# Expert blocks of two sizes in a one-core transformer kernel: up to 64 tokens with high and low rows side by side

## The chip, the core and the metric

The kernel runs as one program on 1 core of a Trainium2 chip. The metric is device time in microseconds (us) for one execution. The engines are named as the profile names them: PE multiplies matrices (PEld is its load of the stationary operand), DVE, ACT and POOL work elementwise, SP and the queues ACTq and POOLq issue transfers. POOL is also called GpSimd.

## The reference

All of it is float32: 256 tokens of width 1024 pass through an attention block and then through a hybrid layer that ends in a mixture of experts. The change touches only that last part:

```python
scores = jax.nn.sigmoid((t @ w_router).astype(jnp.float32))
_, eidx = lax.top_k(scores + router_bias, 8)          # 8 of 64 experts for each token
g = take_along_axis(scores, eidx, 1); g = g / sum(g) * 2.5
...                                                   # tokens sorted by expert, in blocks of up to 128
def expert_block(e, toks, gs):
    xb = t[toks]
    return (silu(xb @ w1[e]) * (xb @ w3[e])) @ w2[e] * gs[:, None]
out = routed_sum(expert_block) + swiglu(t, ws1, ws3, ws2)
```

`w1` and `w3` are 1024x256 for each expert, `w2` is 256x1024: 3 MB an expert. Evaluated on its own inputs, the reference's routing gives 33 experts any token at all: 17 of them have more than 64 tokens (69 to 124), 16 have 1 to 59, none has more than 128.

## The kernel before

Two thirds of the span are the attention block, the mixing layer and the router; the change leaves them alone. Then the routing code (DVE, L1596 to L1622) counts the tokens of each (expert, half) pair, drops the empty ones and writes a list `work`: the number of blocks, the expert of each, and the column of the table `pcol` that holds its gates and ranks. One block is one expert with up to 128 tokens, 33 of them. They run in a loop that each engine has as a program of its own, unrolled over r = 0 to 3; i is the block's number, and semaphores alone tie the engines together.

To keep float32 accuracy at a fast matmul rate, each operand is split into a high part (`_hi`, rounded by ACT) and a rest (`_lo`, a subtraction on DVE), and a product is three matmuls: hi*hi, hi*lo, lo*hi. For block i:

- PE, "up" (L2074): 8 pieces of 128 rows of w1 and w3 side by side, three products each, 24 matmuls of 512 columns into `hidden_b`. Then it transposes (turns) the gathered rows of block i+1 (L2051, 8 transposes), adds block i-1's result to the output sums (scatter, L2059, two halves of 4 matmuls), turns h (L2089, 2 transposes) between the halves, finds the tokens of block i+2 (L2041), and does "down" (L2101, 12 matmuls).
- ACT: `down_hi` (L1166), two pieces of `up_hi` of block i+1 (L1149), silu (L1174), the high part of the next rows (L1144), `h_hi` (L1177), the other two pieces of `up_hi`, `y_hi` (L1185).
- DVE: two `down_lo` (L1667), two `up_lo` (L1642), the product with silu (L1672), the rest of the next rows (L1636), `h_lo` (L1675), gates and tokens (L1628, L1629), two more `up_lo`, two `y_lo` (L1684).
- POOL: `pick` (L899), a comparison that selects the tokens of block i+2; `put` (L929), the matrix that scatters block i's rows, from a row of `place_rows` that SP broadcast to all partitions (L754); and the gather of 128 rows of block i+2 from DRAM (L909).
- SP: loads the weights of block i+2 into the buffer that block i leaves free (L742, L749), after DVE's last `down_lo` of block i.

## Time and profile before

| | us |
|---|---|
| median of 3 runs | 1058.93 |
| lowest, highest | 1056.66, 1059.56 |
| span of the profiled execution | 1053.0 |
| first matmul of block 0, first matmul of block 32 | 656.73, 1029.93 |

The span runs from the first instruction to the last; the time of a run also holds what lies around it. The page gives busy time per engine. Lists by window give, for a stretch, the busy us and the number (x) of instructions of PE, PEld, DVE, ACT and POOL, the granted PE clock (1.00 is 2.4 GHz, 0.5 is 1.2 GHz), the share of the 16 transfer engines and GB/s. A timeline row gives the start, the duration, engine, line, operation, output<-inputs, shape and how many instructions stand in the row (x2). In brackets is the idle time before it and who ended it. A matmul's duration is from start to its last result; the next one starts before that, so the rate is read from the starts.

### The profile page before, as it was taken

How to read it: one execution, taken by the hardware profiler on the slowest of the kernel's cores; microseconds unless marked ns; L12 is line 12 of the kernel's file. 1: busy time of each engine (PE TensorE's matmuls, PEld its weight loads, DVE VectorE, ACT ScalarE, POOL GpSimd, SP SyncE). 2: the span in 40 equal slices, each digit the busy share in tenths (PEclk: the TensorE clock that was granted, in tenths of full speed). 3: DMA queues.
4: the chain of work that ended last, by engine and by line, in shares of the span. 5: the costliest groups of instructions: out<-in, count | busy, mean ns of one | idle time of the engine just before them, and what ended most of it. 6: DMA issues, size and time to landing. Idle time of an engine off the chain costs nothing. (4 is left out here: it accounts for less than half of the span.)

```text
span 1053.0 us, 16530 instructions
## 1 busy us (share of the span) xinstructions
PE 1003.7 (95%) x5182; PEld 810.2 (77%) x5182; DVE 787.6 (75%) x1310; ACT 584.7 (56%) x895; POOL 287.9 (27%) x355
## 2 busy tenths in 40 slices
PE   8999999999999899989879989999999999999996
PEld 7778777778766676778768876778888888888885
DVE  4677888768844543566775654899999999999997
ACT  4554664445433342435425423777777777777774
POOL 5154452224100000041226113322322232233222
PEclk9999999999999999999989999999999999999999
DMA  9877777768635243536242316888888888788884
GB/s 315 277 260 257 225 237 274 234 201 283 211 99 180 96 160 120 171 93 232 88 153 88 101 60 259 313 307 321 341 327 313 334 332 329 306 340 341 325 314 179
DMA packets 85349, 247.39 MB, mean 235 GB/s; under 512 B 13276, under 2 KB 23957, under 8 KB 71986
## 3 DMA queue, kind: packets, MB, share of 16 engines
q1 hardware_dynamic: 71042, 201.19, 53.3%
q0 software_dynamic: 13680, 45.13, 12.0%
q8 instruction: 29, 0.48, 0.2%
q10 hardware_dynamic: 576, 0.41, 0.1%
q14 instruction: 22, 0.18, 0.1%
HBM read 244.27 MB, written 2.29 MB: 234 GB/s over the span
## 5 line engine op out<-in xcount | busy, mean ns | idle before, releaser
L1804 PE MATMUL bank<-w_hi,a_hi 128*128 128x512 f32 (+2 forms) x512 | 205.3, 401 | 10.0 <-DVE w_lo L1266 4.5
L1804 PE MATMUL bank<-w_hi,a_lo 128*128 128x512 f32 (+2 forms) x512 | 196.5, 384 | 0.0
L1804 PE MATMUL bank<-w_lo,a_hi 128*128 128x512 f32 (+2 forms) x512 | 196.2, 383 | 0.0
L1266 DVE TENSOR_TENSOR w_lo<-ring,w_hi 128x1024 fp32r<-128x1024 f32 (+2 forms) x132 | 152.7, 1181 | 50.4 <-ACT w_hi L989 46.5
L989 ACT ACTIVATE w_hi<-ring 128x1024 fp32r<-128x1024 f32 (+2 forms) x140 | 141.0, 1023 | 73.9 <-PE bank L1804 70.2
L1642 DVE TENSOR_TENSOR up_lo<-raw_weights,up_hi 128x1024 fp32r<-128x1024 f32 x136 | 164.4, 1250 | 3.0
L1149 ACT ACTIVATE up_hi<-raw_weights 128x1024 fp32r<-128x1024 f32 x136 | 135.8, 1050 | 0.1
L1804 PEld LDWEIGHTS bank<-w_hi,a_hi 128*128 128x128 f32 x512 | 96.2, 188 | 39.4 <-issue 17.6
L1804 PEld LDWEIGHTS bank<-w_hi,a_lo 128*128 128x128 f32 x512 | 96.2, 188 | 19.8
L1804 PEld LDWEIGHTS bank<-w_lo,a_hi 128*128 128x128 f32 x512 | 96.4, 188 | 18.2 <-issue 1.4
L2074 PE MATMUL bank<-up_hi,x_block_hi 128*128 128x512 f32 x264 | 105.1, 398 | 1.0 <-issue 1.0
L2074 PE MATMUL bank<-up_lo,x_block_hi 128*128 128x512 f32 x264 | 104.9, 397 | 0.0
L2074 PE MATMUL bank<-up_hi,x_block_lo 128*128 128x512 f32 x264 | 104.9, 397 | 0.0
L929 POOL TENSOR_SCALAR put<-block_rows,consts 128x256 fp32r<-128x256 f32 x33 | 30.5, 924 | 246.6 <-PE bank L2059 127.4
L820 POOL DMA_DIRECT2D merged<-in_w_ada_dram x96 | 53.2, 557 | 127.4 <-DVE ada_acc L1405 94.1
L800 POOL TENSOR_SCALAR mean_squares<-mean_squares 128x8 f32<-128x8 f32 (+2 forms) x32 | 10.4, 325 | 279.0 <-ACT logits L942 199.0
L1667 DVE TENSOR_TENSOR down_lo<-raw_weights,down_hi 128x1024 fp32r<-128x1024 f32 x66 | 77.9, 1222 | 7.3 <-ACT down_hi L1166 7.2
L1405 DVE SCALAR_TENSOR_TENSOR ada_acc<-merged,c_col,ada_acc 128x512 f32<-128x512 f32 x84 | 62.8, 748 | 6.4 <-DMA merged<-in_w_ada_dram 3.5
L1166 ACT ACTIVATE down_hi<-raw_weights 128x1024 fp32r<-128x1024 f32 x66 | 66.0, 1050 | 0.3 <-issue 0.3
L1185 ACT ACTIVATE y_hi<-bank,block_gates 128x512 fp32r<-128x512 f32 x66 | 45.5, 689 | 31.3 <-PE bank L2101 30.9
L2074 PEld LDWEIGHTS bank<-up_hi,x_block_hi 128*128 128x128 f32 x264 | 50.0, 189 | 13.2 <-issue 1.2
L2074 PEld LDWEIGHTS bank<-up_hi,x_block_lo 128*128 128x128 f32 x264 | 50.1, 190 | 12.0
(264 smaller groups left out, 1926.5 us busy)
## 6 DMA issues: line engine op xcount, KB each, us to landing
raw_weights<-in_w_dram SPq DMA_DIRECT2D x102, 1024.0 KB, 7.0
ring<-in_w_in_dram SPq DMA_DIRECT2D x58, 1024.0 KB, 5.8
merged<-in_w_ada_dram POOLq DMA_DIRECT2D x96, 256.0 KB, 4.2
ring<-in_w_out_dram SPq DMA_DIRECT2D x8, 1024.0 KB, 5.9
ring<-in_w_branch_dram SPq DMA_DIRECT2D x6, 1024.0 KB, 4.9
bias<-rel_rows SPq DMA_DIRECT2D x40, 128.0 KB, 5.2
block_rows<-place_rows SPq DMA_DIRECT2D x34, 128.0 KB, 8.7
ring<-in_ws_dram SPq DMA_DIRECT2D x2, 1024.0 KB, 5.3
```

The source lines that it names most:

```text
L820: gp.dma_start(ada_row(q), src).then_inc(S(f"ada_loaded_{q % ADA_SLOTS}"), 16)
L929: gp.tensor_scalar(put[:, :], row4[:, r, :], consts[:, C_COL:C_COL + 1], None, ALU.is_equal)\
L989: act.activation(w_parts[0][:, 2 * p:2 * p + 2, 0:w], view(j, kind)[:, 2 * p:2 * p + 2, :], ACT.Copy)\
L1149: act.activation(up_hi[:, r % 2, 4 * kh:4 * kh + 4, m, :], raw_up(raw[:, 1 - r % 2, :], kh, m), ACT.Copy)\
L1166: act.activation(down_hi[:, f, :], raw[:, 1 - r % 2][:, UP + f * DM:UP + (f + 1) * DM], ACT.Copy)\
L1185: act.activation(y_hi[:, hf * CH:(hf + 1) * CH], y_b[hf][:, :], ACT.Copy, scale=gcol[:, r, 0:1])\
L1266: dve.tensor_tensor(w_parts[1][:, 2 * p:2 * p + 2, 0:w], view(JOB[it[1:3]], kind)[:, 2 * p:2 * p + 2, :], w_parts[0][:, 2 * p:2 * p + 2, 0 ...
L1405: dve.scalar_tensor_tensor(out=o, in0=ada_row(q), scalar=c_col[:, 1, k:k + 1], in1=o, op0=ALU.mult, op1=ALU.add) .then_inc(S("ada_step" if ...
L1642: dve.tensor_tensor(up_lo[:, r % 2, 4 * kh:4 * kh + 4, m, :], raw_up(raw[:, 1 - r % 2, :], kh, m), up_hi[:, r % 2, 4 * kh:4 * kh + 4, m, : ...
L1667: dve.tensor_tensor(down_lo[:, f, :], raw[:, 1 - r % 2][:, UP + f * DM:UP + (f + 1) * DM], down_hi[:, f, :].bitcast(F32), ALU.subtract).th ...
L1804: mm = pe.matmul(ps[:, 0:wide], a_parts[za][:, k, t * P:(t + 1) * P], w_parts[zw][:, k, 0:wide], start=start, stop=stop)
L2074: mm = pe.matmul(hidden_b[:, :], (xe_hi, xe_lo)[zx][:, k, :], (up_hi, up_lo)[zw][:, r % 2, k].rearrange("p m n -> p (m n)"), start=(k == 0 ...
```

## The change

Blocks alternate. A block with an even number takes up to 128 tokens, as before. A block with an odd number ("half") takes up to 64: its rows are gathered as 64, and the high part stands in columns 0 to 63 and the rest in columns 64 to 127 of one stationary operand. So two matmuls (with `up_hi`, with `up_lo`) stand in for three, 16 instead of 24 in "up" and 8 instead of 12 in "down". After "up", rows 64 to 127 of the result have to be added to rows 0 to 63 (an ACT copy to `hidden_sum`, a DVE addition). The routing sorts experts into large and small and interleaves them: large ones at even places, small ones at odd places; what is left of the longer list follows. An odd place with no small expert would run as an empty block. `put` is now made from the token column `tok_f` and a constant row, so `place_rows`, its broadcast and the transposes that made it are gone. One of the four `up_lo` pieces of each block moves from DVE to POOL, behind the gather. In a half block both halves of the scatter come before the transposes of h.

The core of the diff (DVE and PE helpers in the order of the file):

```diff
+HALF = P // 2
+UP_PIECES = ((0, 0), (0, 1), (1, 0))
...
-                sp.dma_start(row4[:, r, :], place_rows[bass.ds(v, 1), :].to_broadcast([P, TOK])).then_inc(S(f"row_loaded_{r}"), 16)
...
+                at = S_HALF if r % 2 else S_TOK
                 for t in range(NT):
-                    gp.tensor_scalar(pick[:, r % 2, t, :], consts[:, C_IOTA:C_IOTA + P], col4[:, r, 4 * t + 3:4 * t + 4].bitcast(F32), None, ALU.is_equal)\
+                    gp.tensor_scalar(pick[:, r % 2, t, :], slots[:, at:at + P], col4[:, r, 4 * t + 3:4 * t + 4].bitcast(F32), None, ALU.is_equal)\
                       .then_inc(S("pick_ready"), 1)
...
+                rows = HALF if r % 2 else P
+                gp.indirect_dma_start(out=xg[0:rows, r % 2, :], out_offset=None, in_=h2_rows,
+                                      in_offset=bass.IndirectOffsetOnAxis(ap=tok[0:rows, r, 0:1], axis=0))\
                   .then_inc(S(f"rows_gathered_{r}"), 16)
+
+            def rest_of_up_weights(i, r):
+
+                gp.wait_ge(S("up_hi"), 4 * i + 4)
+                gp.sem_inc(S("begun"), 1)
+                gp.tensor_tensor(up_lo[:, r % 2, KT // 2:KT, 1, :], raw_up(raw[:, 1 - r % 2, :], 1, 1),
+                                 up_hi[:, r % 2, KT // 2:KT, 1, :].bitcast(F32), ALU.subtract).then_inc(S("up_lo_pool"), 1)
...
-                        gp.wait_ge(S(f"row_loaded_{r}"), 16 * (m4 + 1))
-                        gp.sem_inc(S("pool_begun"), 1)
-                        gp.tensor_scalar(put[:, :], row4[:, r, :], consts[:, C_COL:C_COL + 1], None, ALU.is_equal)\
+                        gp.sem_inc(S("begun"), 1)
+                        gp.tensor_scalar(put[:, :], slots[:, S_TOK:S_TOK + TOK], tok_f[:, r, 0:1], None, ALU.is_equal)\
                           .then_inc(S("put_ready"), 1)
-                        gather_rows(i + 2, after)
+                        gather_rows(i + 2, after, m4 * (BODY // 2) + (r + 2) // 2)
+                        rest_of_up_weights(i + 1, (r + 1) % BODY)
...
+                        rows = HALF if r % 2 else P
+                        if r % 2:
+                            act.wait_ge(S("up_done"), i + 1)
+                            act.activation(hsum[0:HALF, :], hidden_b[HALF:P, :], ACT.Copy).then_inc(S("half_low_copied"), 1)
+                            act.wait_ge(S("half_summed"), m4 * (BODY // 2) + (r // 2 + 1))
+                            gated = hsum[0:HALF, 0:ED]
+                        else:
+                            act.wait_ge(S("up_done"), i + 1)
+                            gated = hidden_b[:, 0:ED]
+                        act.activation(hs[0:rows, 0, :], gated, ACT.Silu).then_inc(S("silu_done"), 1)
+                        round_rows(nxt, m4 * (BODY // 2) + (r + 1) // 2)
                         act.wait_ge(S("h_turned"), i + 1)
-                        act.activation(h_hi[:, :, :], turned_b[:, 0:ED].rearrange("p (f n) -> p f n", f=FT), ACT.Copy)\
-                           .then_inc(S("h_hi_ready"), 1)
+                        act.activation(h_hi[:, :, 0:rows], turned_b[:, 0:FT * rows].rearrange("p (f n) -> p f n", f=FT),
+                                       ACT.Copy).then_inc(S("h_hi_ready"), 1)
...
+                    chain(dve.tensor_scalar(used[:, :], counted, consts[:, C_THR:C_THR + 1], None, ALU.is_gt))
+                    chain(dve.tensor_scalar(kinds[:, 0:1], counted, consts[:, C_THR:C_THR + 1], float(HALF), ALU.subtract,
+                                            ALU.is_gt))
+                    dve.tensor_tensor(kinds[:, 1:2], used[:, :], kinds[:, 0:1], ALU.subtract).then_inc(S("used_ready"), 1)
...
+                    large, small = place[:, 0:1], place[:, 1:2]
+                    n_large, n_small = place[:, 2:3], place[:, 3:4]
+                    chain(dve.tensor_scalar(used_at[:, 0:1], small, 1.0, n_large, ALU.add, ALU.min))
+                    chain(dve.tensor_tensor(used_at[:, 0:1], used_at[:, 0:1], small, ALU.add))
+                    chain(dve.scalar_tensor_tensor(out=used_at[:, 1:2], in0=large, scalar=2.0, in1=used_at[:, 0:1],
+                                                   op0=ALU.mult, op1=ALU.subtract))
+                    chain(dve.scalar_tensor_tensor(out=used_at[:, 1:2], in0=used_at[:, 1:2], scalar=kinds[:, 0:1],
+                                                   in1=used_at[:, 0:1], op0=ALU.mult, op1=ALU.add))
+                    dve.tensor_scalar(order[:, :], consts[:, C_IOTA:C_IOTA + NV], used_at[:, 1:2],
                                       used[:, 0:1], ALU.is_equal, ALU.mult).then_inc(S("order_ready"), 1)
...
-                    dve.wait_ge(S("ranks_turned"), 1)
-                    dve.tensor_copy(prow[:, :], y_b[0][:, 0:TOK]).then_inc(S("rows_turned"), 1)
+                        chain(dve.tensor_copy(pcol[:, 0:NV, 4 * t + 3], ranks[:, t, :]))
+                    chain(dve.tensor_scalar(n_blocks[:, :], place[0:1, 2:3], 2.0, -1.0, ALU.mult, ALU.add))
+                    dve.scalar_tensor_tensor(out=work[0:1, 0:1], in0=place[0:1, 3:4], scalar=place[0:1, 2:3],
+                                             in1=n_blocks[:, :], op0=ALU.add, op1=ALU.max).then_inc(S("work_ready"), 1)
...
+                dve.tensor_copy(tok_f[:, r, :], hidden_b[:, 2:3]).then_inc(S("gates_ready"), 1)
...
+                if r % 2:
+                    dve.wait_ge(S("half_x_hi_ready"), pair + 1)
+                    dve.tensor_tensor(xe_hi[:, :, HALF:P], y_b[0][:, :].rearrange("p (b n) -> p b n", b=KT),
+                                      xe_hi[:, :, 0:HALF].bitcast(F32), ALU.subtract).then_inc(S("half_x_lo_ready"), 1)
+                    return
...
+                if half:
+                    dve.wait_ge(S("half_low_copied"), pair(0) + 1)
+                    dve.tensor_tensor(hsum[0:HALF, :], hidden_b[0:HALF, :], hsum[0:HALF, :], ALU.add)\
+                       .then_inc(S("half_summed"), 1)
                 dve.wait_ge(S("silu_done"), i + 1)
-                dve.tensor_tensor(he, hs[:, 0, :], hidden_b[:, ED:2 * ED], ALU.mult).then_inc(S("h_done"), 1)
-                rest_of_rows(i + 1)
+                dve.tensor_tensor(he[0:rows], hs[0:rows, 0, :], (hsum if half else hidden_b)[0:rows, ED:2 * ED], ALU.mult)\
+                   .then_inc(S("h_done"), 1)
+                rest_of_rows(nxt, pair(1))
                 dve.wait_ge(S("h_hi_ready"), i + 1)
-                dve.tensor_tensor(h_lo[:, :, :], turned_b[:, 0:ED].rearrange("p (f n) -> p f n", f=FT),
-                                  h_hi[:, :, :].bitcast(F32), ALU.subtract).then_inc(S("h_lo_ready"), 1)
+                dve.tensor_tensor(h_hi[:, :, HALF:P] if half else h_lo[:, :, :],
+                                  turned_b[:, 0:FT * rows].rearrange("p (f n) -> p f n", f=FT),
+                                  h_hi[:, :, 0:rows].bitcast(F32), ALU.subtract).then_inc(S("h_lo_ready"), 1)
                 take_tokens(i + 2, (r + 2) % BODY)
-                for m in range(2):
-                    rest_of_up_weights(i + 1, nxt, 1, m)
+                rest_of_up_weights(i + 1, nxt, 1, 0)
...
+                if r % 2:
+                    pe.sem_inc(S("begun"), 1)
+                    for k in range(KT):
+                        mm = pe.transpose(y_b[0][:, k * HALF:(k + 1) * HALF], xg[0:HALF, r % 2, k * P:(k + 1) * P],
+                                          consts[0:HALF, C_ID:C_ID + HALF])
+                    mm.then_inc(S("half_rows_turned"), 1)
+                    return
...
+                if half:
+                    pe.wait_ge(S("half_x_lo_ready"), pair(0) + 1)
                 for k in range(KT):
                     if k % 4 == 0:
-                        pe.wait_ge(S(f"x_lo_ready_{k // 4}"), i + 1)
-                        pe.wait_ge(S("up_lo"), 4 * i + k // 2 + 2)
-                    for n, (zx, zw) in enumerate(PASSES):
+                        if not half:
+                            pe.wait_ge(S(f"x_lo_ready_{k // 4}"), pair(0) + 1)
+                        pe.wait_ge(S("up_lo"), 3 * i + k // 4 + 2)
+                    if k == 4:
+                        pe.wait_ge(S("up_lo_pool"), i + 1)
+                    passes = PASSES[0:2] if half else PASSES
+                    for n, (zx, zw) in enumerate(passes):
                         mm = pe.matmul(hidden_b[:, :], (xe_hi, xe_lo)[zx][:, k, :],
                                        (up_hi, up_lo)[zw][:, r % 2, k].rearrange("p m n -> p (m n)"),
-                                       start=(k == 0 and n == 0), stop=(k == KT - 1 and n == 2))
+                                       start=(k == 0 and n == 0), stop=(k == KT - 1 and n == len(passes) - 1))
...
+                    if half:
+                        scatter(1, i).then_inc(S("block_done"), 1)
...
+                    pe.wait_ge(S("h_lo_ready"), i + 1)
                 for hf in range(2):
-                    pe.wait_ge(S(f"x_lo_ready_{hf}"), i + 2)
-                    for n, (f, zh, zw) in enumerate(DOWN_PASSES):
-                        if hf == 0 and n == 2 * FT:
+                    if half:
+                        pe.wait_ge(S(f"x_lo_ready_{hf}"), pair(1) + 1)
+                    elif hf == 0:
+                        pe.wait_ge(S("half_x_lo_ready"), pair(1) + 1)
+                    passes = DOWN_PASSES[0:2 * FT] if half else DOWN_PASSES
+                    for n, (f, zh, zw) in enumerate(passes):
+                        if not half and hf == 0 and n == 2 * FT:
                             pe.wait_ge(S("h_lo_ready"), i + 1)
                         mm = pe.matmul(y_b[hf][:, :], (h_hi, h_lo)[zh][:, f, :],
                                        (down_hi, down_lo)[zw][:, f, hf * CH:hf * CH + CH],
-                                       start=(n == 0), stop=(n == len(DOWN_PASSES) - 1))
+                                       start=(n == 0), stop=(n == len(passes) - 1))
```

On DVE, one trip of the loop before, with the semaphores each row waits for (`hT` is h before it is turned):

```order
L1667 TENSOR_TENSOR down_lo<-raw_weights,down_hi 128x1024 [waits down_hi]
...
L1642 TENSOR_TENSOR up_lo<-raw_weights,up_hi 128x4x256 [waits up_hi]
L1672 TENSOR_TENSOR hT<-hs,bank 128x256 [waits silu_done]
L1634 REGISTER_ALU
L1636 TENSOR_TENSOR x_block_lo<-bank,x_block_hi 128x512 [waits x_hi_ready_0]
L1636 TENSOR_TENSOR x_block_lo<-bank,x_block_hi 128x512 [waits x_hi_ready_1]
L1675 TENSOR_TENSOR h_lo<-bank,h_hi 128x256 [waits h_hi_ready]
```

And in a half block of the changed kernel, the same place:

```order
L1687 TENSOR_TENSOR up_lo<-raw_weights,up_hi 128x4x256 [waits up_hi]
L1718 ISA
L1719 TENSOR_TENSOR hidden_sum<-bank,hidden_sum 64x512 [waits half_low_copied]
L1722 TENSOR_TENSOR hT<-hs,hidden_sum 64x256 [waits silu_done]
L1679 ISA
L1681 TENSOR_TENSOR x_block_lo<-bank,x_block_hi 128x512 [waits x_hi_ready_0]
L1681 TENSOR_TENSOR x_block_lo<-bank,x_block_hi 128x512 [waits x_hi_ready_1]
L1726 TENSOR_TENSOR h_hi<-bank,h_hi 128x2x64 [waits h_hi_ready]
```

The addition stands behind the two `up_lo` and ahead of the product; the rows of the next block, a full one, still come ahead of h's rest.

On PE, from the transposes of h to "down" in a half block (both halves of the scatter stand ahead of the first row here):

```order
L2156 MATMUL bank<-consts,hT 128x64 [waits h_done]
L2156 MATMUL bank<-consts,hT 128x64
L2087 ISA
L2089 MATMUL bank<-block_cols,pick 128x4 [waits pick_ready]
L2089 MATMUL bank<-block_cols,pick 128x4
L2162 ISA [waits h_hi_ready]
L2167 ISA [waits h_lo_ready,down_lo]
L2174 MATMUL bank<-down_hi,h_hi 128x512 [waits x_lo_ready_0]
```

"Down" of a half block waits for h's rest before its first matmul; before, the wait for it stood at the fifth. On POOL, one trip of the changed loop, with a new last row:

```order
L903 TENSOR_SCALAR pick<-slots,block_cols 128x128 [waits tokens_product]
L903 TENSOR_SCALAR pick<-slots,block_cols 128x128
L941 TENSOR_SCALAR put<-slots,block_tokens_f 128x256 [waits slots_loaded,block_done]
L909 REGISTER_ALU [waits h2_stored]
L911 ISA [waits tokens_ready]
L914 DMA x_gathered<-h_rows,block_tokens 64x1024 [waits half_rows_turned]
L920 ISA
L922 TENSOR_TENSOR up_lo<-raw_weights,up_hi 128x4x256 [waits up_hi]
```

The next `pick` stands behind that piece.

## Rows read from the trace of the kernel before

**Rows 1.** The page: span, and busy time by engine.
```profile
span 1053.0 us, 16530 instructions
PE 1003.7 (95%) x5182; PEld 810.2 (77%) x5182; DVE 787.6 (75%) x1310; ACT 584.7 (56%) x895; POOL 287.9 (27%) x355
```
**Rows 2.** Line L2074, "up": count, durations, first and last start.
```profile
L2074 PE MATMUL bank<-up_hi,x_block_lo x264: 388/397/628, 657.7 to 1035.3; 128*128 128x512 f32 x132
```
**Rows 3.** By window: the first matmuls, then the loop.
```profile
656.70:660.20 3.50, 3.47 (x8) 2.81 (x9) 2.96 (x4) 3.50 (x4) 0.00 (x0) 0.51 1.01 415
660.20:1029.90 369.70, 368.00 (x1777) 301.76 (x1776) 341.23 (x444) 281.50 (x380) 115.25 (x125) 1.00 0.85 325
```
**Rows 4.** Timeline of PE over one block, 797.7 to 810.
```profile
797.78 0.39 PE L2074 MATMUL bank<-up_hi,x_block_hi 128*128 128x512 f32 x1
...
803.37 1.05 PE L2051 MATMUL bank<-consts,x_gathered 128*128 128x128 f32 x8
804.18 0.47 PE L2059 MATMUL bank<-y_hi,put 128*128 128x512 f32 x1
...
805.20 0.39 PE L2089 MATMUL bank<-consts,hT 128*128 128x128 f32 x2
...
806.49 0.48 PE L2101 MATMUL bank<-down_hi,h_hi 128*128 128x512 f32 x1
...
809.34 0.39 PE L2074 MATMUL bank<-up_hi,x_block_hi 128*128 128x512 f32 x1
```
**Rows 5.** The same block on ACT, DVE, POOL and SP.
```profile
799.68 2.36 DVE L1667 TENSOR_TENSOR down_lo<-raw_weights,down_hi 128x1024 fp32r<-128x1024 f32 x2 [0.23 <-ACT down_hi L1166]
...
801.96 2.35 DVE L1642 TENSOR_TENSOR up_lo<-raw_weights,up_hi 128x1024 fp32r<-128x1024 f32 x2
...
802.87 0.82 SPq L742 DMA_DIRECT2D raw_weights<-in_w_dram  x2
...
803.57 0.38 ACT L1174 ACTIVATE hs<-bank 128x256 f32<-128x256 f32 x1 [1.07 <-PE bank L2074]
...
804.02 1.09 ACT L1144 ACTIVATE x_block_hi<-bank 128x512 fp32r<-128x512 f32 x2
...
804.24 0.41 DVE L1672 TENSOR_TENSOR hT<-hs,bank 128x256 f32<-128x256 f32 x1
...
804.65 1.29 DVE L1636 TENSOR_TENSOR x_block_lo<-bank,x_block_hi 128x512 fp32r<-128x512 f32 x2
...
805.62 0.38 ACT L1177 ACTIVATE h_hi<-bank 128x256 fp32r<-128x256 f32 x1 [0.51 <-PE bank L2089]
...
806.04 0.42 DVE L1675 TENSOR_TENSOR h_lo<-bank,h_hi 128x256 fp32r<-128x256 f32 x1
...
807.78 1.37 POOL L909 DMA_INDIRECT x_gathered<-h_rows,block_tokens  x1 [0.16 <-issue]
```
**Rows 6.** POOL's rest of weights beside DVE, around 526.
```profile
524.20 9.61 POOL L859 TENSOR_TENSOR w_lo<-ring,w_hi 128x1024 fp32r<-128x1024 f32 x4 [6.08 <-ACT w_hi L989]
```
**Rows 7.** DVE there, and line L1561 in all.
```profile
526.69 2.37 DVE L1561 TENSOR_TENSOR selmask<-score,consts 128x128 f32<-128x128 f32 x1
L1561 DVE TENSOR_TENSOR selmask<-score,consts x2: 431/1398/2365, 526.7 to 539.8; 128x128 f32<-128x128 f32 x1, 128x256 f32<-128x256 f32 x1
```
**Rows 8.** Block 1: POOL's picks beside DVE's weight work; one late pick.
```profile
671.11 4.77 POOL L899 TENSOR_SCALAR pick<-consts,block_cols 128x128 fp32r<-128x128 f32 x2
...
673.05 2.45 DVE L1642 TENSOR_TENSOR up_lo<-raw_weights,up_hi 128x1024 fp32r<-128x1024 f32 x2
```
**Rows 9.** Waits over the loop, 660 to 1043: PE's for gathered rows.
```profile
PEld bank L2051 <- DMA x_gathered<-h_rows,block_tokens: 7.2, 20, 1.0
```
**Rows 10.** Transfers from 804 to 812, then from 812 to 815, by queue.
```profile
q1 hardware_dynamic: 412, 3.07, 96.0%
...
q0 software_dynamic: 144, 0.52, 43.0%
```
**Rows 11.** DVE in the routing: a small step, and the copy for `place_rows`.
```profile
633.10 0.22 DVE L1596 TENSOR_SCALAR used<-bank,consts 128x1 f32<-128x1 f32 x1 [0.99 <-PE bank L2019]
...
637.57 0.42 DVE L1619 COPY prow<-bank 128x256 f32<-128x256 f32 x1
```

More of the change, by code:

```diff
@@ L512, in build @@
         ranks = sb("ranks", [P, NT, NV], F32, routing)
[L513 removed]
         gsum = sb("gsum", [P, NT], F32, routing)
         used = sb("used", [NV, 1], F32, routing)
[L516 removed]
+        kinds = sb("kinds", [NV, 2], F32, routing)
+        used_at = sb("used_at", [NV, 2], F32, routing)
+        place = sb("place", [NV, 4], F32, routing)
+        n_blocks = sb("n_blocks", [1, 1], F32, routing)
         order = sb("order", [NV, NV], F32, routing)
@@ L1655, in _, with expert_block @@
             take_tokens(1, 1)
-            for kh in range(2):
-                for m in range(2):
-                    rest_of_up_weights(0, 0, kh, m)
-            rest_of_rows(0)
-            dve.wait_ge(S("work_ready"), 2)
+            for kh, m in UP_PIECES:
+                rest_of_up_weights(0, 0, kh, m)
+            rest_of_rows(0, 0)
+            dve.wait_ge(S("work_ready"), 3)
             n_work = dve.value_load(work[0:1, 0:1], min_val=0, max_val=MAX_WORK)
-            def expert_block(i, r):
+            def expert_block(i, r, pair):
                 nxt = (r + 1) % BODY
+                half = r % 2
+                rows = HALF if half else P
                 for f in range(FT):
@@ L2085, in expert_block @@
                     scatter(0, i)
+                    if half:
+                        scatter(1, i).then_inc(S("block_done"), 1)
                 pe.wait_ge(S("h_done"), i + 1)
+                rows = HALF if half else P
+                if half:
+                    pe.sem_inc(S("begun"), 1)
                 for f in range(FT):
-                    mm = pe.transpose(turned_b[:, f * P:(f + 1) * P], he[:, f:ED:FT], ident)
+                    mm = pe.transpose(turned_b[:, f * rows:(f + 1) * rows], he[0:rows, f:ED:FT], consts[0:rows, C_ID:C_ID + rows])
                 mm.then_inc(S("h_turned"), 1)
-                if not first:
+                if not first and not half:
                     scatter(1, i).then_inc(S("block_done"), 1)
```

133 lines of the change are left out of this document (68 added, 65 removed).

## The prediction

> **What bounds the kernel now.** I read the page first: PE is busy 95% of the span [rows 1]. The change sits in the block loop, so the next view is line L2074: its first and last starts are 377.6 us apart, which is 32 blocks and 21 matmuls (21 x 0.23), so a block takes (377.6 - 4.9)/32 = 11.65 us on average [rows 2]. The window of the loop says who fills it: PE 368.0 of 369.7 us, DVE 341.2 (92%), ACT 281.5, the transfer engines 0.85 [rows 3]. PE is the bound, and DVE and the transfers stand close behind, so less PE work pays only as far as these let it.
>
> The timeline of one block gives the budget [rows 4]. From 797.78 to 809.34 are 11.56 us: "up" 24 matmuls in 5.59 (0.233 each), transposes of rows 0.81, then 2.31 with 8 scatter matmuls, h's transposes and the token search, "down" 12 matmuls in 2.85 (0.2375 each). The 0.09 us to the mean are blocks in which PE waits for gathered rows, 7.2 us in 20 waits, most of them in the first blocks [rows 9].
>
> The same block on the others is the view that decides [rows 5]. Times are from the block's first matmul. DVE starts `down_lo` at +1.90, because ACT must first round the last block's y and then `down_hi`. Four subtractions follow without a gap, and the product with silu starts at +6.46, though silu was done at +6.17. So in a full block DVE is already level with PE there: the transposes of h stand at +7.42.
>
> **The change part by part.** The reference's routing has 17 experts above 64 tokens and 16 below. They interleave exactly: 33 blocks as before, 17 full and 16 half, none empty.
>
> *Half block, PE alone.* 16 x 0.233 + 0.81 + 2.31 + 8 x 0.2375 = 8.75 us, 2.8 less than now. If that were all, 16 halves would save 45 us.
>
> *Half block, the chain through DVE.* The start at +1.90 and the four subtractions stay, since the piece that went to POOL is the fourth of `up_lo`, which lies later. So the new addition cannot start before +6.46, while PE has ended "up" at +3.7. From there, each step by its nearest row [rows 5]: addition of 64x512, as one of the two `x_block_lo`, 0.65; silu 0.38; product 0.41; with some 0.1 of handover this is +8.0. DVE then does the rows of the next full block, 1.29, which ends at +9.35 (ACT's 1.09 behind silu keeps ahead of it). h's transposes and `h_hi` lie inside that: PE to ACT took 0.42 (805.20 to 805.62), `h_hi` under 0.38. h's rest, half as wide as the 0.42 of today, is 0.3: +9.65, and PE can begin "down" at +9.75. 1.90 more gives **11.65 us**. The ACT copy of rows 64 to 127 (about 0.6) lies in ACT's present gap before silu and costs nothing; without that gap it would add its 0.6. Bounds: 11.3, if the 64-partition steps are shorter by a third and handovers vanish, and 12.1, if each of the seven handovers costs 0.1 more than I allow.
>
> *Picks.* POOL's next `pick` pair now runs behind the piece, so beside DVE's subtractions instead of ahead of them. That was seen once, in block 1: the picks took 4.77 us for two, and DVE's two `up_lo` 2.45 instead of 2.35 [rows 8, 5]. I take twice 0.1 for the two, +0.2 on the half block: 11.85. The picks end near +7 and PE asks for them after +8, so their own lateness is covered.
>
> *Full block.* It keeps all products. The rows that it turns are the 64 of the next half: 8 transposes of 64 columns instead of 128, 0.81 to some 0.55; bounds 0.4 and 0.81. The addition does not occur, `x_block_lo` is one step instead of two. 11.56 - 0.26 = **11.3 us** (11.15 to 11.56).
>
> *Transfers.* Today 3.07 MB of weights go by themselves at 96% until 812, and the gather's 0.52 MB comes behind them by 815 [rows 10]. The issue at +5.1 hangs on DVE, so it stays. Without the broadcast and with every second gather halved, the load falls from 0.85 of the time. The rows of a full block are wanted at +3.7 of the half before it and land near +4.9, but that half waits for DVE until +8.0 anyway. The waits of [rows 9] should nearly vanish.
>
> *POOL's piece.* 2.4 us each [rows 6]. It starts behind the gather, about +11.2, and ends near +2.1 of the next block. PE wants it at its ninth or thirteenth "up" matmul, +1.9 in a half (slack there), +2.8 in a full block. What it does to DVE is in the trace: beside four such pieces in a row a DVE operation of two SBUF inputs took 2.37 us where a wider one of the same line took 0.43, and the wait was as long as the piece beneath it [rows 6, 7]. So whichever comes second waits. DVE's `down_lo` wants to start at +1.9, about when the piece lets go. I take 0 for it, and put the risk in a rival.
>
> The Trainium skill, SBUF — State Buffer, section "SBUF: two separate sides", says that the pair of ports shared by VectorE and GpSimd is an exclusive lock held for a whole instruction, between a VectorE operation with two SBUF inputs and a GpSimd one that reads SBUF. The 2.37 us of [rows 7] agrees. By that rule DVE would wait for the last 0.2 to 0.3 us of every piece, 33 x 0.25 = 8 us on top of the sum.
>
> *Routing.* Before the first block, eight small DVE steps come in (kinds, places, number of blocks) at 0.22 each, one behind the other, and the copy of 0.42 goes [rows 11]. They lie on the path to `work`, whose readers start the first weights: +1.3 us (bounds 0.8 and 2).
>
> *Sum.* 16 pairs of 11.3 + 11.85 = 370.4 against 32 x 11.65 = 372.8: -2.4. With the routing +1.3: -1.1. The profiled execution, 1053.0, would have a span of 1051.9; the runs stand 5.9 above that span in their median, so I forecast **1057.8 us**: no change that can be told, since 0.3% (3.2 us) is about what a measurement tells from none.
>
> **The rivals.**
>
> *A. The half block becomes what PE needs (faster).* If DVE's start moved forward, a half would fall to DVE's own work in it (341.2 us over the 31.7 blocks of [rows 3] are 10.8 each, less 1.2 for the piece, plus 0.65 for the addition: 10.2). 16 x 1.65 = 26 less: 1033. For it: PE's 2.8 us. Against: DVE's first subtraction follows ACT's `down_hi`, which follows the end of "down"; nothing in the change shortens this. A weak form, both bounds low (11.15 + 11.3 + 0.1): 16 x 0.75 = 12 less, +1.3, so 1048. Together 0.25.
>
> *B. POOL's piece and DVE collide (slower).* Its place is the start of a block, its price the piece's 2.4 us or a part. It decides when the gather ends after +11.4, or when a half falls below 11.5: then the piece still runs at +1.9 and all four subtractions, the addition and "down" shift with it. If it comes even later, DVE's subtractions are already running, and POOL has to wait for them as the picks did [rows 8], and PE for `up_lo_pool`. At 0.5 us a block it costs 33 x 0.5 = 16: 1074. At 1 us in halves and fulls alike, 1091. For it: the margin is only some 0.1 us. Against: DVE works on PSUM just while the piece runs. 0.23.
>
> *C. Longer handovers (slower).* The upper bound of the half, 12.1 + 0.2, and 11.56 for the full: 16 x 0.56 = 9, +1.3: 1069. Between that and the sum lies 1063. 0.12.
>
> *D. The clock.* In the half PE idles some 3 us, in two or three pieces. The granted clock was 0.51 from 656.7 to 660.2, behind a start with long gaps, and 1.00 in all of the loop [rows 3]. If a half fell to 1.2 GHz for 3.5 us, it would lose about half of that: 16 x 1.7 = 27, 1086. No single gap should be above 1.3 us. 0.03.
>
> *E. The lists don't interleave.* With one large expert fewer the blocks stay 33; with each two more, an empty half of 11.85 us comes in. The router rounds as before; 0.01.
>
> **How the numbers follow.** The forecast 0.36, A 0.25, B 0.23, C 0.12, D and E 0.04. The likeliest one's own range is 1054 to 1063. The range that should hold 8 in 10 leaves out the strong form of A and the heavy collisions: 1044 to 1078. Faster by over 0.3%: A and the lower edge of the forecast's own range, 0.28. Within 0.3%: 0.32. Slower by over 0.3%: B, C, D, E and the upper edge, 0.40.
>
> **What would show it.** In the profile after: 16 matmuls of "up" in every second block, the period alternating 11.3 and 11.85; in a half, DVE's addition at +6.5 and PE idle ahead of h's transposes and again ahead of "down"; `up_lo` on POOL of 2.4 us ending before DVE's `down_lo`. I am wrong if the addition starts well before +6.4, if `down_lo` starts past +2.1 or takes over 1.4 us for one, if POOL's piece starts past the next block's start, or if the granted clock in the loop is below 1.

## The result, and the profile after

| | before | after |
|---|---|---|
| median of 4 runs | 1059.1 | 1095.8 |
| lowest, highest | 1056.66, 1059.56 | 1092.33, 1097.52 |
| block loop (first matmul of block 0 to that of block 32) | 373.2 | 411.4 |
| behind the loop | 23.0 | 22.3 |

The ratio is 1.0347 (95%: 1.0325 to 1.037): slower. Forecast was 1057.8, with a range up to 1078. The two medians differ by 36.7 us, the two profiled executions by 42.7 (1053.0 and 1095.7). Of these 38.2 lie in the loop. The first matmul of block 0 also stands 5.2 us later: 3.5 of them arise ahead of the routing, in code that the change leaves alone, and most of that is one stretch at 1.2 GHz (from 352.8 on) that the execution of before did not have; 1.7 come from the routing on.

The page of the changed kernel, the same lines as [rows 1] (a group's last numbers are busy us and mean ns of one):
```profile
span 1095.7 us, 16111 instructions
PE 998.1 (91%) x4988; PEld 785.8 (72%) x4988; DVE 766.2 (70%) x1317; ACT 583.8 (53%) x894; POOL 403.8 (37%) x391
...
L1713 DVE TENSOR_TENSOR down_lo<-raw_weights,down_hi 128x1024 fp32r<-128x1024 f32 x66 | 91.7, 1428 | 7.2 <-ACT down_hi L1184 7.2
```
PE has 194 matmuls less than before and only 5.6 us less busy time. The 192 matmuls of "up" and "down" that are gone would be 45 us at before's 0.233 us each, so the others take longer than they did. The window of the loop, with the columns of [rows 3], gives one reason: the mean granted clock is 0.93 where before had 1.00. (The "up" matmuls with the rest of the rows number 136, which is 17 x 8: there are 17 full blocks and 16 halves, as forecast, and rival E is out.) Then four stretches of one block's end and the next one's start:
```profile
661.92:1073.30 411.38, 362.77 (x1592) 278.85 (x1593) 322.53 (x448) 283.49 (x382) 226.66 (x159) 0.93 0.73 276
...
936.30:939.90 3.60, 2.96 (x16) 2.26 (x16) 3.04 (x4) 1.08 (x4) 0.49 (x2) 1.00 0.57 177
939.90:943.28 3.38, 2.21 (x10) 1.84 (x11) 2.88 (x7) 2.83 (x6) 1.41 (x2) 1.00 1.01 427
943.28:946.68 3.40, 3.40 (x9) 2.64 (x8) 2.13 (x3) 2.86 (x4) 3.37 (x3) 0.50 1.04 377
946.68:950.00 3.32, 3.32 (x16) 2.67 (x15) 3.32 (x4) 2.18 (x3) 2.46 (x2) 1.00 0.08 15
```
From 943.28 to 946.68 the granted clock is 0.50 (1.2 GHz): 9 matmuls where the next stretch has 16. Ahead of it PE was idle for a third of one stretch (2.21 us busy of 3.38) and a fifth of the one before. There are 16 such stretches of 3.4 us in the loop, 54.6 us in all; before had one, in block 0, where the changed kernel has one too.

Now the half block that ends there, beside [rows 4, 5], from the timeline of the changed kernel. Its PE:
```profile
931.17 0.40 PE L2136 MATMUL bank<-up_hi,x_block_hi 128*128 128x512 f32 x1
...
933.46 0.50 PE L2136 MATMUL bank<-up_hi,x_block_hi 128*128 128x512 f32 x1 [0.26 <-POOL up_lo L922]
...
936.30 1.09 PE L2106 MATMUL bank<-consts,x_gathered 128*128 128x128 f32 x8 [0.71 <-DMA x_gathered<-h_rows,block_tokens]
...
939.97 0.42 PE L2156 MATMUL bank<-consts,hT 64*128 64x64 f32 x2 [0.70 <-DVE hT L1722]
...
941.80 0.49 PE L2174 MATMUL bank<-down_hi,h_hi 128*128 128x512 f32 x1 [1.10 <-DVE h_hi L1726]
...
944.14 0.63 PE L2136 MATMUL bank<-up_hi,x_block_hi 128*128 128x512 f32 x1
```
And POOL and DVE of the same stretch:
```profile
929.66 1.30 POOL L914 DMA_INDIRECT x_gathered<-h_rows,block_tokens  x1 [0.21 <-issue]
...
931.00 2.41 POOL L922 TENSOR_TENSOR up_lo<-raw_weights,up_hi 128x1024 fp32r<-128x1024 f32 x1
...
933.04 2.92 DVE L1713 TENSOR_TENSOR down_lo<-raw_weights,down_hi 128x1024 fp32r<-128x1024 f32 x2 [0.20 <-ACT down_hi L1184]
933.36 2.99 POOL L903 TENSOR_SCALAR pick<-slots,block_cols 128x128 fp32r<-128x128 f32 x2
...
935.88 2.44 DVE L1687 TENSOR_TENSOR up_lo<-raw_weights,up_hi 128x1024 fp32r<-128x1024 f32 x2
...
938.25 0.67 DVE L1719 TENSOR_TENSOR hidden_sum<-bank,hidden_sum 64x512 f32<-64x512 f32 x1
...
941.23 0.28 DVE L1726 TENSOR_TENSOR h_hi<-bank,h_hi 128x128 fp32r<-128x128 f32 x1
...
943.78 2.40 POOL L922 TENSOR_TENSOR up_lo<-raw_weights,up_hi 128x1024 fp32r<-128x1024 f32 x1
```
In offsets from 931.17: `down_lo` starts at +1.87, as forecast, but POOL's piece runs until +2.24, and the two subtractions take 2.92 us where [rows 5] has 2.36. The addition stands at +7.08 (forecast 6.46), h's transposes at +8.80, "down" at +10.63 (forecast 9.75). PE idles at four places. Three of them come back in every half, the one for the gathered rows in most. The waits over the loop of the changed kernel (us in total, times, longest):
```profile
PE bank L2156 <- DVE hT L1722: 19.4, 19, 1.6
PE bank L2174 <- DVE h_hi L1726: 17.4, 16, 1.1
PE bank L2136 <- POOL up_lo L922: 6.1, 16, 2.1
PE bank L2106 <- DMA x_gathered<-h_rows,block_tokens: 5.1, 9, 1.0
...
PEld bank L2106 <- DMA x_gathered<-h_rows,block_tokens: 11.2, 15, 1.4
```
Before had none of the first three. The last row is the one to hold against [rows 9] (7.2 us in 20 waits): the wait for gathered rows has grown, and it now stands in the halves.

The routing did what was forecast. `used` to `work` is 6.41 us, where before had 5.28, so +1.1 (forecast 1.3); from `work` to the first matmul it is 0.6 more. The first small step, as in [rows 11]:
```profile
636.56 0.22 DVE L1622 TENSOR_SCALAR used<-bank,consts 128x1 f32<-128x1 f32 x1 [0.99 <-PE bank L2071]
```

### The profile page after: what moved, and what is told of

Read it like the earlier page. It is cut to its first block and busy times, and to the rows that moved or that the text cites. A ratio compares the mean times of both kernels' runs of the same rounds, so it can differ in the third digit from the quotient of the medians.

```text
span 1095.7 us, 16111 instructions
## 1 busy us (share of the span) xinstructions
PE 998.1 (91%) x4988; PEld 785.8 (72%) x4988; DVE 766.2 (70%) x1317; ACT 583.8 (53%) x894; POOL 403.8 (37%) x391
## 3 DMA queue, kind: packets, MB, share of 16 engines
q0 software_dynamic: 12656, 40.87, 11.3%
## 5 line engine op out<-in xcount | busy, mean ns | idle before, releaser
L1687 DVE TENSOR_TENSOR up_lo<-raw_weights,up_hi 128x1024 fp32r<-128x1024 f32 x102 | 126.5, 1267 | 0.9 <-ACT up_hi L1167 0.5
L2136 PE MATMUL bank<-up_hi,x_block_hi 128*128 128x512 f32 x264 | 109.9, 416 | 8.2 <-POOL up_lo L922 6.1
L2136 PE MATMUL bank<-up_lo,x_block_hi 128*128 128x512 f32 x264 | 108.0, 409 | 0.0
L1713 DVE TENSOR_TENSOR down_lo<-raw_weights,down_hi 128x1024 fp32r<-128x1024 f32 x66 | 91.7, 1428 | 7.2 <-ACT down_hi L1184 7.2
L903 POOL TENSOR_SCALAR pick<-slots,block_cols 128x128 fp32r<-128x128 f32 x70 | 87.4, 1260 | 22.4 <-DMA block_cols<-pcol 22.4
L1735 DVE SCALAR_TENSOR_TENSOR y_lo<-bank,block_gates,y_hi 128x512 fp32r<-128x512 f32 x66 | 49.5, 751 | 52.4 <-ACT y_hi L1211 52.2
L922 POOL TENSOR_TENSOR up_lo<-raw_weights,up_hi 128x1024 fp32r<-128x1024 f32 x34 | 81.8, 2406 | 0.9
L941 POOL TENSOR_SCALAR put<-slots,block_tokens_f 128x256 fp32r<-128x256 f32 x33 | 31.4, 953 | 134.2 <-issue 134.2
L2174 PE MATMUL bank<-down_hi,h_hi 128*128 128x512 f32 x132 | 64.1, 486 | 18.0 <-DVE h_hi L1726 17.4
L2136 PEld LDWEIGHTS bank<-up_hi,x_block_hi 128*128 128x128 f32 x264 | 52.5, 199 | 27.8 <-POOL up_lo L922 13.0
```

Of the source, the lines that this page charges most:

```text
L903: gp.tensor_scalar(pick[:, r % 2, t, :], slots[:, at:at + P], col4[:, r, 4 * t + 3:4 * t + 4].bitcast(F32), None, ALU.is_equal)\
L922: gp.tensor_tensor(up_lo[:, r % 2, KT // 2:KT, 1, :], raw_up(raw[:, 1 - r % 2, :], 1, 1), up_hi[:, r % 2, KT // 2:KT, 1, :].bitcast(F32), ...
L1687: dve.tensor_tensor(up_lo[:, r % 2, 4 * kh:4 * kh + 4, m, :], raw_up(raw[:, 1 - r % 2, :], kh, m), up_hi[:, r % 2, 4 * kh:4 * kh + 4, m, : ...
L1713: dve.tensor_tensor(down_lo[:, f, :], raw[:, 1 - r % 2][:, UP + f * DM:UP + (f + 1) * DM], down_hi[:, f, :].bitcast(F32), ALU.subtract).th ...
L1735: dve.scalar_tensor_tensor(out=y_lo[:, c], in0=y_b[hf][:, :], scalar=gcol[:, r, 0:1], in1=y_hi[:, c].bitcast(F32), op0=ALU.mult, op1=ALU.s ...
L2136: mm = pe.matmul(hidden_b[:, :], (xe_hi, xe_lo)[zx][:, k, :], (up_hi, up_lo)[zw][:, r % 2, k].rearrange("p m n -> p (m n)"), start=(k == 0 ...
```

## The experiments

Theory after the comparison: (1) POOL's piece (the `up_lo` subtraction that moved there) and DVE hold each other up, about 0.6 us a block; (2) the idle time that this leaves in halves makes the clock fall, and that costs some 15 us more; (3) without both the half block would be near its forecast. Rivals: the clock alone does it; the half's chain through DVE alone; the new `put`. All times below are medians; the loop is that of the profiled execution. "Full" and "half" are the two kinds of block, and lengths of blocks are the usual ones. Ratios are to the kernel before on the same chip.

**e2_no_piece.** The changed kernel, with the fourth piece of `up_lo` on DVE again.
```diff
-UP_PIECES = ((0, 0), (0, 1), (1, 0))
+UP_PIECES = ((0, 0), (0, 1), (1, 0), (1, 1))
...
-                        rest_of_up_weights(i + 1, (r + 1) % BODY)
```


> The changed kernel with the fourth up_lo piece given back to DVE (POOL has pick, put and gather alone). Theory 1 (piece and DVE collide): DVE's two down_lo take 2.36 again instead of 2.7 to 2.9, the addition of the half starts at +6.5 instead of +7.1, the waits of PE for up_lo on POOL (19 us in sum, 32 times) go, the half is 11.9 or less at full clock and there are fewer stretches at 1.2 GHz: 1072 to 1082. Theory 2 (the addition's chain alone, and the clock): the start of the addition moves, but PE idles as long and the clock falls as often: 1088 to 1095. Theory 3: DVE has too much to do with four pieces (10.9 a block, 11.4 in a half) and the time is above 1098.

Measured: 1067.4, ratio 1.0078 (1.0061 to 1.0095), loop 384.8: below theory 1's range. Halves take 11.92 us at full clock, fulls 11.52. One half on DVE and PE:
```profile
986.06 0.40 PE L2131 MATMUL bank<-up_hi,x_block_hi 128*128 128x512 f32 x1
...
987.93 2.36 DVE L1709 TENSOR_TENSOR down_lo<-raw_weights,down_hi 128x1024 fp32r<-128x1024 f32 x2 [0.20 <-ACT down_hi L1180]
...
992.48 0.68 DVE L1715 TENSOR_TENSOR hidden_sum<-bank,hidden_sum 64x512 f32<-64x512 f32 x1
...
994.26 1.29 DVE L1677 TENSOR_TENSOR x_block_lo<-bank,x_block_hi 128x512 fp32r<-128x512 f32 x2 [0.20 <-ACT x_block_hi L1158]
...
996.04 0.49 PE L2169 MATMUL bank<-down_hi,h_hi 128*128 128x512 f32 x1 [1.10 <-DVE h_hi L1722]
```
The addition is at +6.42, as forecast; "down" at +9.98 and not +9.75, since `x_block_lo` began 0.2 late behind ACT and the handover to PE took more. So the piece costs 28 us of the 36.7, what it does to the clock included (16 stretches at 1.2 GHz with it, 6 without). The line of `down_lo` (shortest/median/longest ns) shows the collision by itself. Without the piece:
```profile
L1709 DVE TENSOR_TENSOR down_lo<-raw_weights,down_hi x66: 1214/1222/1228, 662.6 to 1049.4; 128x1024 fp32r<-128x1024 f32 x66
```
In the changed kernel:
```profile
L1713 DVE TENSOR_TENSOR down_lo<-raw_weights,down_hi x66: 1209/1224/3473, 662.3 to 1076.4; 128x1024 fp32r<-128x1024 f32 x66
```

**e5_warm_light and e1_warm.** The changed kernel, with small matmuls that add zeros in a half, where PE waits: 2, 4 and 4 of them in the code (e1: 6, 10 and 8), ahead of the turn of the rows, of h's transposes and of "down". In the trace each stands as two matmuls of 0.11 us from start to start, so e5 adds 20 to a half (2.2 us) and e1 adds 48 (5.3 us), twice what the expectations reckon.
```diff
+                if half:
+                    stay_warm(4)
                 pe.wait_ge(S("h_done"), i + 1)
```


> The changed kernel, plus small matmuls without dependents on PE in half blocks only: 6 before the rows are turned, 10 before the transposes of h, 8 before down. They add zeros to an output sum, so only PE's idle time is filled. Theory 1 (the clock): in the profile after, PE falls to 1.2 GHz some 14 times in the loop because the half blocks leave it idle, and blocks that meet no such stretch are 12.58 (half) and 11.52 (full). With the gaps filled the granted clock stays 1.00 in the loop and 16 pairs of 24.1 to 24.4 replace the 411.4 us of the loop by 386 to 391: 1070 to 1076. Theory 2 (the chain alone): the half is bound by DVE, the slow matmuls lie in time that PE would have waited anyway, and the time stays at 1090 to 1098. Theory 3: the fillers push real work back by themselves: 24 of 0.11 us, up to 2.6 us a half where they do not fit, above 1100.

> As e1_warm with fewer fillers in the half blocks: 2, 4 and 4 instead of 6, 10 and 8 (0.11 us each as e1_warm's trace has them), few enough to fit in the idle time of the changed kernel (0.7, 0.7 and 1.1 us). Theory 1 (the clock costs the changed kernel what its slow blocks show): the granted clock stays 1.00 in the loop, halves take 12.6 to 12.9, fulls 11.5: 1073 to 1080, against 1095.8 of the changed kernel. Theory 2 (the slow stretches lie in time that is lost anyway): the clock may stay up and the time is 1090 to 1098 all the same.

Measured: e1 1112.4, ratio 1.0501; the clock stayed up but for one stretch in block 1, yet so many fillers are work themselves (halves 15.0 us), so it told nothing of the price. e5: 1081.35, ratio 1.0222 (1.0191 to 1.0253), loop 397.3, just above theory 1's range because fulls do not return to 11.5. Its loop window, and the fillers:
```profile
662.40:1059.70 397.30, 380.99 (x1912) 301.61 (x1913) 331.72 (x447) 284.20 (x382) 249.57 (x158) 1.00 0.75 285
...
L2123 PE MATMUL bank<-ones,zeros x320: 269/275/414, 680.8 to 1057.5; 128*128 128x128 f32 x160
```
With fewer stretches at 1.2 GHz (3.4 us in all) the loop is 14.1 us shorter than the changed kernel's, more matmuls notwithstanding. Of the 14.1, 1.5 are the stretch in block 0, which e5 lacks. What stays is the collision at full clock: halves 12.59, fulls mostly 12.0 to 12.3, against 11.92 and 11.52 in e2. That is 0.6 us a block, in both kinds. The fillers don't lengthen the halves: those halves of the changed kernel that kept the full clock take 12.58 to 12.61. The fulls behind them take 11.9 to 12.1 there, so up to some 2 us of e5's loop may be the fillers'.

**e3_put_only and e4_put_piece.** The kernel before, whole blocks only, with `put` built from the token column; e4 adds POOL's piece behind the gather.
```diff
-tensor_scalar(put[:, :], row4[:, r, :], consts[:, C_COL:C_COL + 1], ...)
+tensor_scalar(put[:, :], slots[:, S_TOK:S_TOK + TOK], tok_f[:, r, 0:1], ...)
...
+                        rest_of_up_weights(i + 1, (r + 1) % BODY)   # e4
```


> The kernel before with only the scatter matrix made from the token column and a constant row: no place_rows, no broadcast, no transposes of the ranks, one small DVE copy more a block. If the broadcast ahead of the gather was what PE waited for (8.2 us in 22 waits in the loop), these waits go and the loop falls by 2 to 4 us, the routing by 0.4: 1054 to 1057. If the gather is late for another reason: 1058 to 1060.

> The run before this one (scatter matrix from the token column, all 33 blocks of the full size) plus the fourth up_lo piece on POOL. Theory 1: the collision delays DVE's down_lo by 0.3 to 0.6 a block, but a full block's DVE has 0.5 of room before the transposes of h, so this is 0 to 4 us slower than that run. Theory 2: each block pays the delay: 33 x 0.5 = 16 us slower. Theory 3 (faster): DVE was the hidden bound and the piece frees it: 2 to 5 us faster.

Measured: e3 1053.5, ratio 0.9946 (0.9929 to 0.9962); e4 1062.5, ratio 1.0036 (1.0022 to 1.0049). In e3 the blocks from block 5 on are 11.55 us each and the waits of [rows 9] shrink:
```profile
PEld bank L2043 <- DMA x_gathered<-h_rows,block_tokens: 1.3, 2, 0.7
```
e4 has the collision with no half block in sight, 0.28 us a block and 9 us in all, between its theories 1 and 2:
```profile
L1673 DVE TENSOR_TENSOR down_lo<-raw_weights,down_hi x66: 1210/1392/2146, 660.8 to 1041.6; 128x1024 fp32r<-128x1024 f32 x66
```

**e6_piece_early.** The changed kernel, with the piece moved to where POOL sits idle: it takes the second piece of `up_lo` behind the picks, ahead of `put` and gather, and DVE takes the fourth.
```diff
-UP_PIECES = ((0, 0), (0, 1), (1, 0))
+UP_PIECES = ((0, 0), (1, 0), (1, 1))
...
                         make_pick(i + 2, after, m4 + 1 + (r + 2) // BODY)
+                        rest_of_up_weights(i + 1, (r + 1) % BODY)
```


> The changed kernel with another piece on POOL at another place: the second of the four up_lo pieces, behind the picks and ahead of put and gather, so it can run from +4.8 of a block, when ACT has rounded it, and not at a block's start. DVE has only three subtractions before the addition. Theory 1 (what hurt was where the piece stood, beside down_lo): no stretched down_lo (2.36), the addition of the half starts at +5.4, but its product with silu reads two SBUF inputs and can wait for the piece until +7.6, so the half is 11.5 to 12.0; DVE's work is 9.9 a block: 1050 to 1066. Theory 2 (any such piece on POOL costs DVE its own 2.25 us somewhere): 1080 or more, and DVE operations with two SBUF inputs are stretched elsewhere.

Measured: 1061.4, ratio 1.0033 (1.0001 to 1.0065), loop 373.1: 34 us less than the changed kernel, with as many subtractions on each engine in another order. `down_lo` is at 1.2 us each again. But the half still takes 11.55, though DVE reaches the addition at +5.32. The timeline of a half says why:
```profile
981.74 2.78 POOL L922 TENSOR_TENSOR up_lo<-raw_weights,up_hi 128x1024 fp32r<-128x1024 f32 x1 [3.73 <-ACT up_hi L1167]
...
983.37 1.42 DVE L1721 TENSOR_TENSOR hT<-hs,hidden_sum 64x256 f32<-64x256 f32 x1 [0.48 <-ACT hs L1200]
```
The product reads two SBUF tiles and lasts until just behind the piece's end (984.52), 1.42 us for 0.42.

**e7_piece_early_psum, e9_early_psum_only, e10_early_order_only.** e9 is e6 with the sum of the two products written back to PSUM, so addition and product have one SBUF input each; e10 is e6 with the second scatter behind h's transposes in halves too; e7 has both.
```diff
-dve.tensor_tensor(hsum[0:HALF, :], hidden_b[0:HALF, :], hsum[0:HALF, :], ALU.add)
+dve.tensor_tensor(hidden_b[0:HALF, :], hidden_b[0:HALF, :], hsum[0:HALF, :], ALU.add)
...
-                    if half:
-                        scatter(1, i).then_inc(S("block_done"), 1)
...
-                if not first and not half:
+                if not first:
                     scatter(1, i).then_inc(S("block_done"), 1)
```


> e6_piece_early, and the addition of the half writes its sum back to PSUM, so that silu and the product read PSUM and no DVE step between the third subtraction and h's rest has two SBUF inputs; and PE has h's transposes between the halves of the scatter again, as in a full block. Theory 1: addition at +5.4, product at +6.5, down at +8.7, half 10.6 to 11.0, full 11.5 (or a gather wait of up to 0.5); with the clock up 1035 to 1045, with the clock falling in halves 1045 to 1055. Theory 2: the gathered rows are late for the half (they landed near +4.9) and the transfers (0.85 busy at 11.65 us a block) bound it: half 11.3, 1048 to 1055.

> e6_piece_early with one of e7's two edits: the sum of the half block's two products is written back to PSUM, so the addition and the product with silu have one SBUF input each; TensorE's order stays as in the changed kernel. Theory P (the port): in e6 the product with silu starts at +6.5 but h's transposes come only at +8.05, because a DVE operation of two SBUF inputs waits for POOL's piece that runs beside it; e7 had them at +7.0. So this edit alone gives nearly all of e7: loop near 358 us, halves 10.8, time 1042 to 1045. Theory O (the order): the gain came from putting the second scatter behind h's transposes; then this run stays at e6, halves 11.8, time 1055 to 1062.

> e6_piece_early with the other edit of e7 alone: in a half block the second scatter comes behind h's transposes on TensorE, as in a full one; the sum stays in SBUF. Theory P: the product stays held by POOL's piece, halves 11.7 to 11.8, time 1055 to 1062 as e6. Theory O: halves 10.8 and 1042 to 1045. A third, that the second scatter did nothing but fill a gap and taking it away only moves work behind the transposes: halves up to 0.4 longer, 1062 to 1068.

| | time | ratio (95%) | loop | usual half |
|---|---|---|---|---|
| e6 | 1061.4 | 1.0033 (1.0001 to 1.0065) | 373.1 | 11.55 |
| e9 | 1051.4 | 0.9928 (0.991 to 0.9946) | 365.4 | 11.15 |
| e10 | 1056.0 | 0.9976 (0.9958 to 0.9994) | 370.6 | 11.52 |
| e7 | 1042.3 | 0.9861 (0.983 to 0.9891) | 357.7 | 10.67 |

Neither theory held alone: e9 missed theory P's 1042 to 1045, e10 fits theory P and excludes theory O. With the product free but the second scatter ahead of the transposes, PE itself was late (h's transposes at +7.87), not least because it had waited 1.0 us for the gathered rows: from one half of e9 to the next, the length follows that wait (10.97 with 0.85, 11.14 with 1.03, 12.21 with 2.09); with the order mended but the product held, DVE was (+8.03). Both together give +7.02 and 0.9 us a half, where the single edits give 0.4 and nothing. The product's line in e7 has no long case any more, though the piece runs beside it as before:
```profile
L1721 DVE TENSOR_TENSOR hT<-hs,bank x33: 411/420/423, 666.8 to 1024.5; 128x256 f32<-128x256 f32 x17, 64x256 f32<-64x256 f32 x16
```
What is left in e7's halves is nearly all one wait, for the gathered rows of the next full block; no run here moves the gather:
```profile
PE bank L2106 <- DMA x_gathered<-h_rows,block_tokens: 17.8, 16, 2.2
```
e7 is the fastest kernel of the study, 14.6 us under before (1056.9 on that chip). Its clock stays at full speed in the loop:
```profile
660.55:1018.20 357.65, 335.06 (x1592) 263.02 (x1593) 305.00 (x447) 282.57 (x383) 203.13 (x159) 1.00 0.83 315
```

**e8_no_piece_psum.** e2 with e7's two last edits: is the piece needed at all?

> e2_no_piece with the sum in PSUM and the order of PE in halves as in a full block, no piece on POOL. If the length of the half is the chain of DVE's four subtractions, addition, silu, product (e2: 11.93 at full clock), little moves: half 11.8 to 11.95. The second half of the scatter now stands in the wait for h's rest, so PE idles in other places; if the clock falls less for it, 1060 to 1064, if not 1066 to 1069.

Measured: 1062.65, ratio 1.0051 (1.0026 to 1.0076), loop 379.9, halves 11.75 at full clock. It is: DVE's fourth subtraction ahead of the addition is worth 1.1 us a half. The clock is in the difference too: e8 has five stretches at 1.2 GHz in the loop, e7 none.

**e11_put_piece_early.** e4 with the piece in e6's place, no half blocks.

> The kernel before with put from the token column (as e3_put_only) and POOL's piece, but the second of up_lo, run behind the picks as in e6, so no half blocks. It tells what of e7's gain is the halves' and what is the piece's. Theory H (the halves are what pays): all blocks full and bound by TensorE at 11.5 us, loop 368 to 370, time 1052 to 1054 as e3, so e7's further 10 us are the half blocks. Rival S (DVE's relief pays): DVE one subtraction shorter ahead of the product lets every block fall to 11.2, loop near 358, time near 1043, and the half blocks bring nothing by themselves. Rival L: the product reads one SBUF input here, but down_lo or the picks collide with the piece as in e4: 11.8 a block, 1060.

Measured: 1055.2, ratio 0.9968 (0.9954 to 0.9982), loop 370.8, blocks of 11.55 from block 5 on. Theory H: DVE's relief brings nothing where PE is the bound (ratio 0.0022 above e3's). So what e7 has over e3, 9 us by the ratios and 11.9 in the loop, is the half blocks', and they give it only with the piece in the right place.

## Why the prediction was wrong

The loop, by parts, forecast 370.4 and measured 411.4:

| part | from | us |
|---|---|---|
| fulls 11.52, not 11.3 | e2, 16 x 0.22 | +3.5 |
| halves 11.92, not 11.85 | e2, 16 x 0.07 | +1.1 |
| the piece against DVE, at full clock | e5 397.3, less 16 x (11.52 + 11.92) = 375.0 | +22.3 |
| the clock | changed kernel less e5 | +14.1 |
| sum | | 41.0 |

The table takes each kind of block at its usual length; block 0 and block 1, which differ, are in the last two parts.

*POOL's piece: the step that failed.* The sum gave the piece nothing. "I take 0 for it" rested on the piece ending near +2.1 and DVE starting at +1.9, "about when the piece lets go". The two numbers were nearly right (+2.24, +1.87), and already they don't fit: DVE's first subtraction waits. What the working left out is that the delay feeds itself. `down_lo` late by 0.5 makes the half's gather late (+11.42), so the next piece starts behind the next block's first matmul (+0.19 in e5) and ends at +2.6 there. POOL's picks, which wait behind the piece, then run beside DVE's subtractions and hold these up by some 0.1 more. Measured are 0.6 us a block, and 22 us with block 1 (15.3 us in e5; 13.6 in e2, of which 1.5 are a stretch at 1.2 GHz); rival B had named mechanism, place and its 0.5 us (1074), with a chance of 0.23. A margin of 0.1 us that a chain of 11 us must keep, block after block, should have made this the forecast.

The rule of the Trainium skill, SBUF — State Buffer, section "SBUF: two separate sides", agrees with the rows here: a subtraction or product of two SBUF inputs waited (`down_lo` up to 3.47 us, the product of e6 1.41), and the product with one input in PSUM did not (0.42 in e7). The 8 us that the prediction derived from it were the direct wait alone.

*The clock: rival D, taken too small.* Its chance was 0.03, because "No single gap should be above 1.3 us". It was nearly true (up to 1.6 us, in block 1 2.1), but the reason did not hold. In the changed kernel's blocks 7, 13, 21 and 27 no gap of PE was above 1.1 us, and the clock fell; in e7's block 5 PE had a single gap of 2.2 us, and it stayed. The trace of before had the warning. D calls the start ahead of its one stretch at 1.2 GHz one "with long gaps", but PE's only gaps from 640 to that stretch were 0.9 and 1.0 us:
```profile
654.61 1.09 PE L2051 MATMUL bank<-consts,x_gathered 128*128 128x128 f32 x8 [0.86 <-DMA x_gathered<-h_rows,block_tokens]
656.73 0.76 PE L2074 MATMUL bank<-up_hi,x_block_hi 128*128 128x512 f32 x1 [1.02 <-issue]
```
In e2, which has no piece to wait for, it still fell six times. Over the kernels with half blocks, the stretches in the loop mostly grow with PE's idle time in a usual half: one with 0.5 us (e5, in its long block 1), none with 1.1 (e7) and 1.7 (e9), two with 2.0 (e6), one with 2.1 (e10), five with 2.2 (e8), six with 2.4 (e2), 16 with 2.8 (changed kernel). Halves with the same gaps went either way, and so did executions of one kernel: e8's ten runs go from 1055.55 us at a mean granted clock of 0.993 to 1069.24 at 0.978. The price is 14 us, 12.6 without block 0's stretch, near the half of the 27 forecast: in e2 a half with a stretch takes 1.5 us more (D said 1.7), but in the changed kernel the full behind a slowed half is often back at 11.5, free of the piece.

*Half block.* Right in its chain: the addition at +6.42 without the piece (6.46 forecast), "down" at +9.98 (9.75). That 11.92 in all stands so near to 11.85 is in part luck: the forecast was 11.65 for the chain and 0.2 for the picks, and in e2's half no pick runs beside DVE's subtractions. The chain was 0.27 longer, by the two handovers named at e2.

*Full block.* The transposes of 64 columns saved as forecast in part, 0.64 us for 0.81, but the block kept 11.52. In e2 they start 0.33 behind the last "up" matmul, in [rows 4] it was 0.23 (803.14 to 803.37), and h's transposes stand at +7.37 as ever:
```profile
979.90 0.40 PE L2131 MATMUL bank<-up_hi,x_block_lo 128*128 128x512 f32 x1
...
980.23 0.57 PEld L2096 LDWEIGHTS bank<-consts,x_gathered 64*128 64x128 f32 x8 [0.37 <-issue]
...
980.87 0.50 PE L2111 MATMUL bank<-y_hi,put 128*128 128x512 f32 x1
```
Of 0.26 forecast 0.04 arrived; why the start is later stays open.

*Transfers and `put`.* "The waits of [rows 9] should nearly vanish" came true with `put` alone (1.3 us in e3) and not with half blocks (11.2 us in the changed kernel, against 7.2 before). The working had the reason: rows wanted at +3.7 of a half that land near +4.9 (e2 turns them at +4.8). It was right that DVE covers most of this wait as long as the addition stands at +6.4, but it is PE's idle time all the same, and in e7 and e9 it is no longer covered (usual halves there wait 0.8 to 1.1 us for the rows). Over blocks 1 to 31, e3's loop is 2.0 us shorter than before's, near the 33 x 0.09 = 3 of "The 0.09 us to the mean"; e3's whole gain is 0.54%, 5.7 us, and where the rest of it lies stays open.

*Routing.* Right: +1.1 for 1.3.

*Rival A* comes near the end of a mended kernel, by another way: e7's half is 10.67, where A put DVE's own work at 10.2. A wanted an earlier start of DVE; in e7 that start is still +1.87, and one subtraction less stands ahead of the addition. (A's 1033 takes 26 us from the time before, though 1.65 is the distance to the forecast's half: from 1057.8 it would be 1031.)

## What to carry to other kernels

Before work goes to an idle engine, ask at which moment it will run and what the other engine does then, not how idle it is: a piece of the same size cost 28 us in one place (e2) and brought 20 in another (e7 against e8), the clock's part included. A margin of 0.1 us in a loop is a wait, and a wait that delays the next transfer pays again in the next block. When the bound engine is relieved in only part of the blocks, add up its idle pieces and look at the granted clock first: several short gaps were enough to lose some 12 us.
